# A decoder block with expert gathers on one core: what GpSimd waits for, early sums and loads in another order, idle products, pairs at slots 8 to 24, 24 slots by VectorE

## What is computed

```python
mod = silu(c) @ w_ada + b_ada                      # 1024 x 6144: shifts, scales, gates
h = x * (1 + sc1) + sh1
q, k, v = split(h @ w_in)                          # two groups of 8 heads, 64 wide
y = concat(rms_norm(attention_a), rms_norm(attention_b)) @ w_out
x = layer_norm(ALPHA * x + (1 + g1) * y)
h2 = x * (1 + sc2) + sh2
q = h2 @ w_q_peer                                  # 8 expert heads
v1, i1 = top_k(q[..., :64] @ sub_keys[0].T, 16); v2, i2 = top_k(q[..., 64:] @ sub_keys[1].T, 16)
vals, pos = top_k(v1[..., :, None] + v2[..., None, :], 16)
e = i1[pos // 16] * 128 + i2[pos % 16]             # 128 experts for each token
a = gelu(einsum('cd,chkd->chk', h2, u_tab[e])) * softmax(vals)
f = einsum('chk,chkd->cd', a, v_tab[e])
x = layer_norm(ALPHA * x + (1 + g2) * f)
```

## Time and profile before

| | |
|---|---|
| median of three runs | 834.14 us (832.98 to 834.54) |
| the profiled execution | 833.26 us |
| its span, first to last instruction | 831.4 us |
| PE busy | 687.7 us (83%) |
| VectorE (DVE) busy | 586.9 us (71%) |
| ScalarE (ACT) busy | 340.1 us (41%) |
| GpSimd (POOL) busy | 306.2 us (37%) |
| moved by DMA | 323.72 MB, of it 268.45 MB by the gathers |
| mean granted TensorE clock | 0.970 |

### The profile page before, as it was taken

One profiled execution on the slowest core, in us unless ns is written; L12 is line 12 of the kernel. 1 busy time (PEld: TensorE's weight loads), 2 busy tenths in 40 slices (PEclk: granted clock), 3 DMA queues, 4 the chain that ended last, 5 costly groups with the idle time before them and its releaser, 6 DMA issues.

```text
span 831.4 us, 7233 instructions
## 1 busy us (share of the span) xinstructions
PE 687.7 (83%) x2000; PEld 330.8 (40%) x2000; DVE 586.9 (71%) x1296; ACT 340.1 (41%) x988; POOL 306.2 (37%) x263
## 2 busy tenths in 40 slices
PE   6999999799998878786979877777778687878874
PEld 3887745545434444442423323222223232222221
DVE  6645886689689767787777777767576757675545
ACT  0012142376636343434454536344443434343333
POOL 5000000234356535554535444543443434434320
PEclk9999999999999998998898999999999999999998
DMA  9999992399999999999999999999999999999991
GB/s 353 401 419 419 376 388 82 149 401 392 375 394 396 421 421 421 421 421 422 421 422 421 421 421 421 423 421 420 421 422 421 422 422 423 420 421 423 420 422 75
DMA packets 48043, 323.72 MB, mean 389 GB/s; under 512 B 5698, under 2 KB 8066, under 8 KB 9346
## 3 DMA queue, kind: packets, MB, share of 16 engines
q0 software_dynamic: 36864, 268.45, 78.2%
q1 hardware_dynamic: 10258, 54.55, 16.5%
q10 hardware_dynamic: 882, 0.27, 0.1%
HBM read 322.18 MB, written 1.07 MB: 389 GB/s over the span
## 4 chain that ended last, share of the span: by engine, by line
DMA 52%; PE 29%; DVE 8%; ACT 4%; issue 4%; POOL 2%; SPq 0%; DVEq 0%; ACTq 0%
DMA ring<-in_experts,e_all 50%; PE bank L465 14%; PE bank L490 6%; PE bank L456 4%; DVE ring L814 3%; DVE acc L937 2%; POOL ring L1065 2%; ACT diag L660 1%; DMA lnw<-in_w 1%; PE bank L560 1%; PE bank L579 1%; ACT weight L651 1%; DMA ring<-in_w 1%; ACT gel L647 1%; PE bank L521 1%
## 5 line engine op out<-in xcount | busy, mean ns | idle before, releaser
L465 PE MATMUL bank<-ring,diag 128*128 128x512 f32 x952 | 472.3, 632 | 113.4 <-ACT diag L660 112.8
L1065 POOL DMA_INDIRECT ring<-in_experts,e_all x256 | 293.8, 1148 | 490.7 <-PE bank L465 293.4
L465 PEld LDWEIGHTS bank<-ring,diag 128*128 128x128 f32 x952 | 172.8, 196 | 391.5 <-ACT diag L660 236.8
L814 DVE CUSTOM_DVE_ANT_0 ring<-ring,T_h 128x1024 f32<-128x1024 f32 x128 | 156.8, 1226 | 113.0 <-DMA ring<-in_experts,e_all 113.0
L814 DVE CUSTOM_DVE_ANT_0 ring<-ring,h 128x1024 f32<-128x1024 f32 x128 | 156.7, 1224 | 74.0 <-DMA ring<-in_experts,e_all 72.6
L647 ACT ACTIVATE gel<-pre 128x1 f32<-128x1 f32 x256 | 51.9, 203 | 332.4 <-DVE pre L814 331.5
L660 ACT ACTIVATE diag<-consts,weight 128x128 f32<-128x128 f32 x238 | 95.5, 401 | 7.8
L651 ACT ACTIVATE weight<-gel,g_all 128x1 f32<-128x1 f32 x256 | 75.4, 295 | 9.3
L937 DVE SCALAR_TENSOR_TENSOR acc<-ring,cact,acc 128x512 f32<-128x512 f32 x60 | 49.0, 817 | 2.8
L456 PE MATMUL bank<-ring,hT_yT 128*128 128x512 f32 x80 | 35.5, 594 | 0.0
L490 PE MATMUL bank<-hT_yT,lnw 128*128 128x256 f32 x128 | 30.8, 402 | 1.1 <-DVE hT_yT L907 1.1
(11 more groups left out here) (161 smaller groups left out, 570.9 us busy)
## 6 DMA issues: line engine op xcount, KB each, us to landing
ring<-in_w SPq DMA_DIRECT2D x28, 1024.0 KB, 12.9
H_s<-in_w SPq DMA_DIRECT2D x7, 1024.0 KB, 13.8
lnw<-in_w SPq DMA_DIRECT2D x6, 1024.0 KB, 15.6
ring<-in_experts,e_all POOLq DMA_INDIRECT x256
T_h<-scratch SPq DMA_DIRECT2D x1, 2048.0 KB, 25.8
xT_y<-in_xT SPq DMA_DIRECT2D x1, 1024.0 KB, 13.8
x<-in_x SPq DMA_DIRECT2D x1, 1024.0 KB, 16.9
H_s<-in_w SPq DMA_DIRECT2D x2, 512.0 KB, 7.1
```

The source lines that it names most:

```text
L465: last = nc.tensor.matmul(tile_sum(t)[n], diag[:, m % DIAGS, :], ring[:, RING_AT[i], D + CH * n:D + CH * n + CH], start=(s == 0), stop=(s ...
L814: nc.vector.tensor_tensor_reduce(ring[:, r, 0:D], ring[:, r, 0:D], h2[i // SLOTS], 1.0, 0.0, ALU.mult, ALU.add, pre[:, i % PAIR:i % PAIR + ...
L1065: nc.gpsimd.indirect_dma_start(ring[:, r, :], None, A["experts"], bass.IndirectOffsetOnAxis(ap=e_all[:, i:i + 1], axis=0)).then_inc(slot_i ...
```

## The change

It does seven things.

1. GpSimd waits for the very products that empty a place (`empty`), not for ScalarE's `ring_free`; the steps `free` are gone. Its two additions of one to rows of `mod` are gone too: ScalarE adds the one in `madd`.
2. The bias and the first modulation result get banks 6 and 7 (`APART`). PE does two single rows of chunk 2 instead of three, and four idle products of 256 columns (`warm`) stand between the early sums.
3. On SyncE the second output block is loaded ahead of the patches. Chunk 11 comes in patches of 4, 2, 1 and 1 rows, and is summed behind the first layer norm. `wsum` 7 goes ahead of `yT` of the first group.
4. The second copy of values (`vcopy`) is done by ScalarE behind slot 1's weight, and the table of the gelu is loaded ahead of slot 0 (`gelu`).
5. In `BESIDE` the pairs of attention units go from slots 3 to 19 to slots 8 to 24, and what follows them is placed anew. The ring is six places wide up to slot 44, not 36.
6. VectorE sums 24 slots, not 18: those with `i % 16 == 12` too.
7. The gates of the two halves of a projection, and of the expert sum, are each followed by their own addition; PE tells of the first half of a tile's expert sum before the second is done (`half_done`). A query product waits for the second half of its tokens only where it reads them.

```diff
-BY_PE = {2: (3, 6, 7)}
+BY_PE = {2: (3, 7)}
-WIDE_FROM = 36
+WIDE_FROM = 44
...
-    [("qkz", 0, 0), ("qkz", 0, 1), ("qkz", 1, 0), ("wsum", 0), ("bias",), ("qkz", 1, 1), ("modp", 0)] + [("modk", 2, k) for k in BY_PE[2]]
+    [("qkz", 0, 0), ("qkz", 0, 1), ("qkz", 1, 0), ("wsum", 0), ("bias",), ("qkz", 1, 1), ("modz", 0), ("warm", 2), ("modk", 2, 3), ("modp", 0), ("warm", 1),
+     ("modk", 2, 7), ("warm", 1), ("wsum", 2), ("modc", 0), ("qkh", 0, 0), ("qkh", 0, 1), ("wsum", 1), ("modp", 1),
...
-BY_DVE = [i for i in range(16, 112) if i % 16 in (2, 4, 5)]
+BY_DVE = [i for i in range(16, 112) if i % 16 in (2, 4, 5, 12)]
...
-    3: [("S", 6), ("S", 7)], 5: [("Tr", 6), ("Tr", 7)], 7: [("PV", 6), ("PV", 7)], 9: [("S", 8), ("S", 9), ("yT", 1, 1)],
+    8: [("S", 6), ("S", 7)], 10: [("Tr", 6), ("Tr", 7)], 12: [("PV", 6), ("PV", 7)], 13: [("yT", 1, 1)],
...
-PLACE = {s: (n % STEP_BANKS, n // STEP_BANKS) for n, s in enumerate(s for s in FILLS if s not in LATE)}
+APART = [("bias",), ("modc", 0)] + [("wo", 0, 1, n) for n in range(2)]
+PLACE = {s: (n % STEP_BANKS, n // STEP_BANKS) for n, s in enumerate(s for s in FILLS if s not in APART)}
...
+        patches = [H_s[:, 0:2 * D].rearrange("p (k n) -> p k n", n=CH), xT_y[:, D:2 * D].rearrange("p (k n) -> p k n", n=CH), V_x1[:, 1:2, 0:CH],
+                   diag[:].rearrange("p (r i) c -> p r (i c)", r=1)]
...
+            filled(sp, ("qk", 3, 1))
+            load(("out", 1))
             summed(sp, 9)
             sp.wait_ge(hT_ready, KC)
...
-            filled(sp, ("qk", 3, 1))
-            load(("out", 1))
...
+                    if s == SLOTS - 1 and n == 0:
+                        last.then_inc(half_done, 1)
...
+                if kind == "warm":
+                    w = places[W_PLACES[CHUNK[("ada", 0)]]]
+                    arrived(pe, CHUNK[("ada", 0)], 0)
+                    for _ in range(step[1]):
+                        nc.tensor.matmul(bank[STEP_BANKS - 1][:, 0:T], ones[:], w[:, 0, 0:T], start=True, stop=True)
...
+                    if m // 2 == SH2:
+                        evacuate(("modrow", m), part, src[:])
+                    else:
+                        nc.scalar.activation(part, src[:], ACT.Identity, bias=ones[:, 0:1]).then_inc(freed(("modrow", m)), 1)
...
+                elif kind == "gelu":
+                    own.settle()
+                    own.then(nc.scalar.activation(spare[:], epsc[:], ACT.Gelu))
...
-                for n in range(2):
-                    dve.wait_ge(*f[n][2])
+                    dve.wait_ge(*taken)
                     own.then(nc.vector.scalar_tensor_tensor(z[:, halves[n]], res[:, halves[n]], ALPHA,
                                                             acc[:, n, :], ALU.mult, ALU.add, accum_out=lnst[:, i, n:n + 1]))
...
-            pool.wait_ge(rows_in, 16)
-            nc.gpsimd.tensor_scalar(mod[0:1, G1, :], mod[0:1, G1, :], 1.0, None, ALU.add)
-            nc.gpsimd.tensor_scalar(mod[0:1, SC2:G2 + 1, :], mod[0:1, SC2:G2 + 1, :], 1.0, None, ALU.add).then_inc(rows_one, 1)
+            empty = {4: [("v", 1, 1)], 6: [("q", 0, 1)], 0: [("v", 0, 1)], 2: [("wo", 1, g, 0) for g in range(2)]}
...
-                    pool.wait_ge(ring_free, 1 + sum(before is None for before in RING_BEFORE[:i]))
+                    for step in empty[r // 2 * 2]:
+                        filled(pool, step)
```

More of the change, by code:

```diff
@@ L256, in build @@
         junk = sb("junk", [P, D], mybir.dt.bfloat16)
-        diag = sb("diag", [P, DIAGS, P])
         swork = sb("swork", [P, 2, NK])
@@ L502, in _ @@
                     if i == 0:
-                        for late in LATE:
-                            settle_bank(pe, late)
+                        for step_apart in APART:
+                            settle_bank(pe, step_apart)
                     if i == SLOTS:
@@ L510, in _ @@
                     pe.wait_ge(set_ready, 1)
-                    dst, _ = open_bank(("modc", step[1]))
-                    if step[1] == 0:
-                        nc.tensor.matmul(dst[:, 0:2 * KC], nought[:, 0:P], nought[:, 0:2 * KC], start=True, stop=False)
+                    dst = bank[PLACE[("modc", 0)][0]] if step[1] == 0 else open_bank(("modc", 1))[0]
                     column_sums(dst, step[1], step[1] == 0)
+                if kind == "modz":
+                    nc.tensor.matmul(open_bank(("modc", 0))[0][:, 0:2 * KC], nought[:, 0:P], nought[:, 0:2 * KC], start=True, stop=False)
+                if kind == "warm":
[3 more added lines that the diff above has]
+                        nc.tensor.matmul(bank[STEP_BANKS - 1][:, 0:T], ones[:], w[:, 0, 0:T], start=True, stop=True)
                 if kind == "modk":
@@ L783, in add_residual, with gate @@
                                         ALU.add, ALU.mult).then_inc(mean_ready, 1)
-            def gate(t, g):
-                for n in range(2):
-                    half = slice(CH * n, CH * n + CH)
-                    src = filled(dve, ("wo", t, g, n))
-                    nc.vector.scalar_tensor_tensor(acc[:, n, :], src, ystat[:, t, 2, g:g + 1], mod[:, G1, half],
-                                                   ALU.mult, ALU.mult).then_inc(freed(("wo", t, g, n)), 1)
+            def gate(t, g, n):
+                half = slice(CH * n, CH * n + CH)
+                src = filled(dve, ("wo", t, g, n))
+                nc.vector.scalar_tensor_tensor(acc[:, n, :], src, ystat[:, t, 2, g:g + 1], mod[:, G1, half],
+                                               ALU.mult, ALU.mult).then_inc(freed(("wo", t, g, n)), 1)
+                settle_bank(dve, ("wo", t, g, n))
+                return half
             def centre(i, z, gain, dst):
@@ L935, in _ @@
                         own.settle()
-                        row = patches[k // 2][:, k % 2, :] if patched else w[:, k, :]
+                        if patched and patch_of[k] == (1, 0):
+                            dve.sem_inc(patch_read, 1)
+                        row = patches[patch_of[k][0]][:, patch_of[k][1], :] if patched else w[:, k, :]
                         ins = nc.vector.scalar_tensor_tensor(part, row, cact[:, k:k + 1], part, ALU.mult, ALU.add)
@@ L1036, in _ @@
                         settle_bank(dve, ("modrow", m))
-                    f = [(tile_sum(t)[n], (slot_done, PE_SLOTS.index(SLOTS * (t + 1) - 1) + 1), (f_taken, 2 * t + n + 1)) for n in range(2)]
+                    ready = ((half_done, t + 1), (slot_done, PE_SLOTS.index(SLOTS * (t + 1) - 1) + 1))
+                    f = [(tile_sum(t)[n], ready[n], (f_taken, 2 * t + n + 1)) for n in range(2)]
                     add_residual(NT + t, mod[:, G2, :], f, V_x1[:, t, :], V_x1[:, t, :])
```

74 lines of the change are left out of this document (30 added, 44 removed), and 22 rows, old and new, of tables (BESIDE, PLAN).

## The result

The changed kernel takes 840.17 us (median of 20 runs, 837.46 to 842.14), the kernel before 835.57 us beside it (20 runs, 832.59 to 839.32): ratio 1.0055, 95% interval 1.0042 to 1.0069. It is 0.55% slower, where the forecast was 827.4 us. The execution profiled took 842.14 us, and its span is 840.3 us against 831.4 before: 8.9 us are to be found. That is more than the 4.6 us between the medians, since the execution profiled is the slowest of the twenty, and that of the kernel before lies 2.3 us under its median.

A forecast was written before the change was run, and what follows sets the result against it. It took the front, gathers at the transfers' pace (421 GB/s) and a tail to make the time. Terms -2.8 - 1.6 - 1.5 + 0.5 - 0.85 = -6.25 from 833.26 gave 827.0, set at 827.4 us toward the runs' median; range 822.5 to 832.0.

The forecast's parts named there:

- The front: Everything up to the first gather: it starts at 153.4 us, not 156.2; -2.8 us, bounds -0.2 and -4.0.
- The rival of a front that gives nothing: PE waits for a load or its clock stays low, so the front term falls to -0.2: 830.0 us; chance 0.14.
- The tail: After the last gathers: the first half is gated and added while PE works on the second; -0.85 us, bounds -0.4 and -1.2.
- The first slots: Start of the gathers: slot 0's place is free some 5 us sooner; -1.6 us, bounds 0 and -2.4.
- The pairs: Attention pairs moved to slots 8 to 24: less PE and VectorE work beside them; -1.5 us, bounds +1 and -4.
- Slots 25 to 47: Projection, layer norm, two new VectorE sums and the ring's six places until slot 44 fall here: +0.5 us, bounds -0.5 and +4.
- "Nothing" for the four behind slot 48: The other four new sums lie where VectorE has room, so cost nothing; 5.1 us if that room were gone.
- My rival of slower sums: All six new VectorE sums come out on the path and shut gathers out, 13.0 us: 840.4 us; chance 0.08.

The follow-up runs named there:

- e1: Changed kernel with VectorE's sums back to 18 from 24: 840.47 us, ratio 1.0066 to the kernel before.
- e3: Changed kernel with VectorE summing no slot before 32 (20 sums left): 839.29 us, ratio 1.0047 to the kernel before.
- f1: Changed kernel with the ring six places wide up to slot 40, not 44: 837.92 us, ratio 1.002 to the kernel before.
- f4: Changed kernel with the steps behind the pairs spread out (projection at slots 33, 37, 42, 46) and six places up to slot 52: 840.36 us, ratio 1.006.
- h1: Changed kernel with only the order of the wide ring's eight places altered, none reused before six slots: 837.65 us, ratio 1.0034 to the kernel before.
- f3: Changed kernel with three idle PE products ahead of the third step (PV) of units 5, 8 and 10: 836.48 us, ratio 1.0017 to the kernel before.
- g1: Changed kernel with the idle products of f3 and six places up to slot 40, as in f1: 834.96 us, ratio 0.9987 to the kernel before.
- h3: Changed kernel, its slot list kept, with the idle products of f3, six places up to slot 42 and 18 sums: 831.94 us, ratio 0.9966.
- h4: e4 with every step from unit 5 to the layer norm's transposes two slots later (pairs at 5 to 21): 830.55 us, ratio 0.9949.
- g3: e4 with VectorE also summing slots 60, 76, 92 and 108: 830.26 us, ratio 0.9936 to the kernel before.
- e4: Changed kernel with the slot list of before, six places up to slot 36 and 18 sums: 827.23 us, ratio 0.9902 to the kernel before.
- e2: Changed kernel with the slot list of before and six places up to slot 36, but 24 sums: 831.66 us, ratio 0.996 to the kernel before.

## Why the prediction was wrong

**The front (-2.8) was right.** First gather at 153.08 us against a forecast of 153.4; on the way the layer norm's result was done at 133.5 us (133.7) and ScalarE's copy of the first queries began at 142.38 (142.6). The 4 us step and the pause near 120 us are gone as said. The rival of a front that gives nothing didn't occur, though the sixteen products did begin at half rate: the cap by the load covered that. **The tail (-0.85)** gave 0.6.

**The first slots (-1.6)** can't be faulted. The gather of slot 6 went out as early as said. In the profiled execution 16 slots took 47.9 us against 47.8, with a granted clock of 0.63 on the mean from 176 to 190 us, behind a pause of 2.47 us ahead of the fifth unit's `PV`. But e1, e3, f1, f4 and h1 do the same up to slot 16, with the same pause, and took 44.1, 45.7, 45.5, 47.2 and 45.3 us. The mean of the six is 45.9, 1.9 us less than the one trace of the kernel before. With the clock held they took 44.5, 45.5 and 44.8 us (f3, g1, h3), so the clock costs about 1 us here. Single traces of this stretch scatter by 3.7 us.

**The pairs (-1.5) failed.** I counted VectorE's routing beside them, and took PE's two slots less as a relief. The step that failed is the overlap on PE: between the second and the third step of a pair PE now has nothing to do for 2.5 us while it waits for the copies of the transposes, the granted clock falls to 0.50, and what follows takes up to twice as long. Slots 16 to 24 took 25.8 us and not less than 23.2, and the 23.2 hold a load of 1 MB that the 25.8 do not. The two slots that PE doesn't sum are only part of the reason, since in e3, which gives them back, one of the two pauses stays. The size is 3.7 us over all (f3), or 3.0 with the ring to 40 (f1 to g1). I had the row that shows it, slot 0's products at half rate behind a pause of 3 us, and used it for the front alone.

**Slots 25 to 47 (+0.5, bounds -0.5 and +4) failed most.** From slot 24 to 64 they lost 8.9 us, or 6.4 without the load that moved behind slot 24. Two steps of this term went wrong. First, I read `WIDE_FROM` 36 to 44 as eight more slots on six places, and never worked out which place each slot gets. The switch at 44 reuses two places after four slots: 2.5 us (h1). Second, I took the projection, the layer norm and the queries as moved with their room. But the four products of the projection went from slots 22 to 28 to slots 31 to 38, and the query of slot 32 ahead of them, to 27, and the list costs 4.7 us with the clock held, no place reused early and 18 sums (h3). Why is not settled. PE is full from 246 to 272 us and the gathers wait for it, which fits work packed too densely. But f4, which spread it, gained nothing, h4 lost 3.3 us with the same spacing two slots later, and h3 loses as much ahead of slot 24 as in slots 24 to 40. The idle products and the six more slots on six places are in the 4.7 us too; no run takes them out.

**The sums.** "Nothing" for the four behind slot 48 is in doubt: g3 is 3.0 us slower than e4, and with all six sums it is 4.4 (e2). That is the measured price of the kernels, but their traces have most of it in slots 0 to 16, so whether the sums themselves cost this is not shown. I inferred room from VectorE's busy share over 200 us, which says nothing of the moment at which a place comes free; GpSimd's waits for such sums do grow, from 27.4 us in e4 to 44.7 in g3 and 52.3 in e2, over the whole run. My rival of slower sums came to the measured time (840.4) by luck and by the wrong mechanism: with 18 sums the changed kernel is as slow (e1). Its reason was misread as well. The gather of 1.83 us began beside a dot product, and the sum started only at 231.60 us. VectorE in the kernel before:

```profile
230.45 1.23 DVE L814 CUSTOM_DVE_ANT_0 ring<-ring,h 128x1024 f32<-128x1024 f32 x1
```

With six more sums the gathers got no longer: 1109 ns on the mean in the changed kernel against 1148 before.

Step by step the 12.9 us between the changed kernel and e4 are: the clock 3.7 (f3), the ring to 40 with the clock held 1.5 (g1), 18 sums and a ring to 42 together 3.0 (h3), and the list with the rest 4.7 (e4). The 3.0 are not divided further; in g1 the gather of slot 40 waits 7.7 us for PE, in h3 1.9, so the ring has a part in them.

The forecast of 827.4 us is what the change gives without its slot schedule and without its six sums (827.23), by chance as much as by reasoning: in e4's trace the front gives 3.3 us and the first slots 2.4, more than the 2.8 and 1.6 that I had given them, and the pairs are where they were. The lower end of my range doesn't follow from its own words either, which give 823.2 and not 822.5.

## What to carry to other kernels

When a ring of buffers changes its size on the way, write down for each slot which place it gets and how many slots ago that place was last used; two places used again after four slots, where the rest have six, held up every later gather, and another order of the same places cured it. When steps are moved, look at what pause that leaves on TensorE, and whether its clock survives it: an idle product in the pause can be worth more than the time it takes. Several edits in one change hide each other's price, so time the parts that touch different stages apart: here the front alone was 1% faster than the kernel before, and the whole 0.5% slower. Ask of each difference between two traces whether it lies where the kernels differ: six kernels with the same first 16 slots took 44.1 to 47.9 us for them. And when loads move, count them in each stretch before comparing its length.

## What the runs showed of the hardware that was not expected

A pause of 2.5 us on TensorE brought the granted clock from 0.99 to 0.50 and made the sixteen records behind it take 3.65 us instead of 1.90, with the four products behind those at 5.24 instead of 3.65; three idle products of 512 columns (2.74 us) kept it. The fall doesn't come at once each time: behind the same pause the sixteen records took 3.65, 3.65, 2.83, 2.17, 2.15 and 1.97 us in six kernels. Nor does holding the clock always pay: in the list of before, the same idle products took away two falls and gave nothing (832.33 against 831.66 us).

In the trace of the kernel before, GpSimd's instruction for a gather took 0.94 us in all 133 cases in which VectorE stood idle when it began, and 1.5 us on the mean, up to 1.99, in the 85 in which it began beside one of VectorE's dot products. This longer instruction did not show in the pace: with 64 slots in 159.7 us the transfers ran at 421 GB/s.
